# Stick-breaking and gate projections in blocks of four heads, tokens in rows

## What is computed

```python
u = _rms(h, norm1_w[l]) * (1.0 + scale1) + shift1
proj = u @ w_in[l].astype(f32)
qa, ka, va, qkv_b, z_b, b_b, a_b, gate_a, gate_b = jnp.split(proj, IN_OFFSETS, axis=-1)

qa = _rms(_heads_2(qa, SB_HEADS, SB_HEAD_DIM), q_norm_w[l])     # 16 heads of 128
ka = _rms(_heads_2(ka, SB_HEADS, SB_HEAD_DIM), k_norm_w[l])
va = _heads_2(va, SB_HEADS, SB_HEAD_DIM)
o_a = _merge_heads(_stick_breaking(qa, ka, va))

qkv_b = jax.nn.silu(_causal_depthwise_conv(qkv_b, conv_w[l]))
qb, kb, vb = jnp.split(qkv_b, (D_GDN_K, 2 * D_GDN_K), axis=-1)  # l2norm of qb and kb follows
o_b = _gated_delta_rule(qb, kb, vb, g, beta)
o_b = _rms(o_b, o_norm_w[l]) * jax.nn.silu(_heads_2(z_b, GDN_HEADS, GDN_V_DIM))

merged = (jax.nn.sigmoid(gate_a) * (o_a @ p_a[l]) + jax.nn.sigmoid(gate_b) * (o_b @ p_b[l]))
h = h + gate1 * (merged @ w_out[l])
```

## Time and profile before

| | |
|---|---|
| median of 3 timed runs | 2782.45 us (2782.1 to 2784.94) |
| the profiled execution | 2780.33 us |
| its span in the profile | 2778.5 us |
| PE busy | 2753.2 us, 99% |
| DVE, ACT, POOL busy | 74%, 52%, 14% |
| mean granted clock of PE | 0.999 |
| HBM read over the span | 612.70 MB, 222 GB/s |

### The profile page before, as it was taken

How to read it: one execution, slowest core, us unless ns; L and a number is a source line. 1 busy time by engine, 2 the same in 40 slices (tenths; PEclk the granted TensorE clock), 3 DMA queues, 4 the chain that set the end, 5 groups by cost and what they waited for, 6 DMA issues and landing times.

```text
span 2778.5 us, 42932 instructions
## 1 busy us (share of the span) xinstructions
PE 2753.2 (99%) x16354; PEld 2384.8 (86%) x16354; DVE 2049.2 (74%) x3589; ACT 1455.5 (52%) x2414; POOL 378.8 (14%) x958
## 2 busy tenths in 40 slices
PE   8999999999999999999999999999999999999999
PEld 4778888888888888888888888888888888888888
DVE  4478877878988787887878877878978555555554
ACT  3465544555566666666666544444454443444443
POOL 0014300000002424344343311000000000000000
PEclk9999999999999999999999999999999999999999
DMA  9956677788755455555555677887858555555554
GB/s 355 354 179 224 228 248 257 275 288 294 279 183 194 163 175 179 176 185 169 178 172 183 220 244 269 310 289 274 280 175 292 188 188 188 193 185 192 186 198 142
DMA packets 179998, 621.84 MB, mean 224 GB/s; under 512 B 20288, under 2 KB 28752, under 8 KB 179152
## 3 DMA queue, kind: packets, MB, share of 16 engines
q1 hardware_dynamic: 169776, 605.62, 63.5%
q10 hardware_dynamic: 10016, 13.47, 1.5%
HBM read 612.70 MB, written 4.21 MB: 222 GB/s over the span
## 4 chain that ended last, share of the span: by engine, by line
PE 84%; DVE 6%; POOL 3%; ACT 3%; issue 2%; DMA 1%; SPq 0%; ACTq 0%; DVEq 0%
PE ps L101 84%; POOL small L116 2%; DVE wlo L116 2%; POOL small L119 1%; PE ps L104 1%; DVE c_y L122 1%; DMA raw<-in_w_s 1%; ACT sb_l L107 1%; ACT whi L107 1%; ACT L110 1%; DMA xc<-in_xc 0%; DVE acc L122 0%; ACT sb_z L107 0%; DVE i_t L116 0%; DVE c_y L119 0%
## 5 line engine op out<-in xcount | busy, mean ns | idle before, releaser
L101 PE MATMUL ps<-act,whi 128*128 128x512 f32 (+1 forms) x6560 | 1612.4, 392 | 1.2 <-DVE act L116 1.2
L101 PEld LDWEIGHTS ps<-act,whi 128*128 128x128 f32 (+1 forms) x6560 | 1191.1, 188 | 230.2 <-issue 5.7
L116 DVE TENSOR_TENSOR wlo<-raw,whi 128x1024 fp32r<-128x1024 f32 (+3 forms) x883 | 1041.7, 1187 | 18.9 <-ACT whi L107 14.4
L107 ACT ACTIVATE whi<-raw 128x1024 fp32r<-128x1024 f32 (+3 forms) x883 | 893.2, 1026 | 167.9 <-PE ps L101 101.5
L101 PE MATMUL ps<-act,wlo 128*128 128x256 f32 (+2 forms) x6416 | 930.8, 290 | 0.2 <-DVE wlo L116 0.2
L101 PEld LDWEIGHTS ps<-act,wlo 128*128 128x128 f32 (+1 forms) x6416 | 836.9, 190 | 37.5 <-issue 9.2
L122 DVE SCALAR_TENSOR_TENSOR acc<-raw,c_act,acc 128x1024 f32<-128x1024 f32 x210 | 268.5, 1279 | 0.0
L119 POOL TENSOR_SCALAR small<-small 128x2 f32<-128x2 f32 (+3 forms) x316 | 137.6, 435 | 935.0 <-DVE small L119 808.8
L116 POOL TENSOR_TENSOR small<-small 128x2 f32<-128x2 f32 (+1 forms) x460 | 162.9, 354 | 348.3 <-ACT u_u L107 314.1
L116 DVE TENSOR_TENSOR w_u<-w_u,ps 128x256 f32<-128x256 f32 x44 | 18.4, 421 | 94.6 <-ACT w_u L107 94.6
L122 DVE SCALAR_TENSOR_TENSOR h_res<-ps,mod,h_res 128x256 f32<-128x256 f32 x64 | 30.9, 484 | 67.6 <-PE ps L101 66.5
(11 more groups left out here) (328 smaller groups left out, 2295.0 us busy)
## 6 DMA issues: line engine op xcount, KB each, us to landing
raw<-in_w_turns SPq DMA_DIRECT2D x754, 512.0 KB, 4.3
raw<-in_w_mods SPq DMA_DIRECT2D x224, 512.0 KB, 4.3
raw<-in_w_s SPq DMA_DIRECT2D x64, 512.0 KB, 6.7
raw<-in_w_turns SPq DMA_DIRECT2D x64, 448.0 KB, 4.3
raw<-in_w_turns SPq DMA_DIRECT2D x32, 384.0 KB, 3.6
raw<-in_w_turns SPq DMA_DIRECT2D x17, 256.0 KB, 3.1
raw<-in_w_kv SPq DMA_DIRECT2D x7, 512.0 KB, 3.4
xc<-in_xc SPq DMA_DIRECT2D x3, 1024.0 KB, 9.6
```

What stands on the lines that cost most here:

```text
L101: return self.e.matmul(*args, **more)
L107: return self.e.activation(*args, **more)
L116: return self.e.tensor_tensor(*args)
```

## The change

The 64 units sq, sk, sv and gz become 16 blocks, bq, bk, bv and bz, each of four heads. A block has eight turns of 128 x 1024 weights again, now two k-tiles of four heads. In them the activations are stationary (128 tokens of L or H) and the weights move, 512 columns at a time, so that tokens come out in rows, the form that the later steps need. Each turn does both halves of the tokens, one ahead of the small matmuls and one behind them (`tokens`), each into its own bank, so that a block holds both banks 7 and 6:

```diff
+        def tokens(turn, half):
+
+            n, u = 16 + turn.t, turn.tiles[0][0]
+            hi, lo, b = HI[n % NH], LO[n % NL], (u.bank, u.other)[half]
+            s = slice(128 * half, 128 * half + 128)
+            e.wait_ge(*on("hi", n))
+            if turn.tiles[0][1] == 0:
+                claim(b)
+            for j, (_, kt) in enumerate(turn.tiles):
+                e.wait_ge(*on(u.rhs, kt))
+                mm(PS[b][:, :], L[:, 0, kt, s], hi[:, 512 * j:512 * j + 512], kt == 0, False)
+                mm(PS[b][:, :], H[:, 0, kt, s], hi[:, 512 * j:512 * j + 512], False, False)
+            e.wait_ge(*on("lo", n))
+            for j, (_, kt) in enumerate(turn.tiles):
+                p = mm(PS[b][:, :], H[:, 0, kt, s], lo[:, 512 * j:512 * j + 512], False, kt == 15)
+            if half:
+                p.then_inc(*tell("pe_gemm", "w_done", n))
+            elif kt == 15:
+                p.then_inc(*tell("pe_block", "first_rows", u.name, u.i))
+            if kt == 15:
+                held[b] = [("rows", u.name, u.i, half)]
...
+            elif turn.block:
+                tokens(turn, 0)
...
+            if turn.block:
+                tokens(turn, 1)
+                continue
```

The order of the stage is new: bk, bq and bv of the first four heads follow one another, and then a block of eight turns alternates with six turns of gq, gk and gv. gq and gk of head 0 go through the late pair of the stage's start instead of sq and sk. The bases of both mixers are set by hand:

```diff
+        block(0, "bk", 0)
...
+        block(rate, "bq", 0)
+        block(rate, "bv", 0)
+        wide = (("bk", 1), ("bz", 0), ("bq", 1), ("bv", 1), ("bk", 2), ("bz", 1), ("bq", 2), ("bv", 2), ("bk", 3), ("bz", 2),
+                ("bq", 3), ("bv", 3), ("bz", 3))
+        for h in range(1, 17):
+            if h <= len(wide):
+                block(rate, *wide[h - 1])
+            else:
+                for _ in range(4):
+                    gate_a(rate)
             if h < 16:
...
+                delta(h, 0)
+                delta(h, 1)
+            delta(h - 1, 2)
...
-        at = e + 19
...
+        at = e + 27
         for h in range(16):
             at = max(self.end("gk", h), at)
             self.base("delta", h, at)
             at += 14
         for h in range(16):
-            self.base("stick", h, (e + 11, e + 20, e + 29, e + 38)[h] if h < 4 else self.end("sk", h) + 3)
...
+            self.base("stick", h, e + ((29, 40, 50)[h] if h < 3 else 62 + 14 * (h - 3)))
```

More of the change, by code:

```diff
@@ L223, in build, with block, delta, gate_a @@
             single(0.5 if n < 12 else 0, "out1", n, (5, 4, 7, 6)[n % 4], "m", src["w_out"][n], two)
[L225 to L228, removed]
+        self.pairs(0, [Unit("g0", x, 5 - x, "raw", range(16), late=x) for x in range(2)], lambda i: w2[48:65:16])
+        ring = itertools.cycle((7, 6))
+        rate = 0.16
+        def block(rate, name, g):
+            first = {"bq": 0, "bk": 16, "bv": 32, "bz": 96}[name] + 4 * g
+            u = Unit(name, g, bank(), "u", range(16))
+            u.other = bank()
+            for k in range(0, 16, 2):
+                self.turn(rate, np.concatenate([w[:, 128 * kt:128 * kt + 128] for kt in (k, k + 1) for w in w2[first:first + 4]], 1),
+                          [(u, k), (u, k + 1)], block=True)
+            self.finish(u)
+        def delta(g, x):
+            single(rate, "g" + "qkv"[x], g, bank(), "u", w2[48 + 16 * x + g], two)
+        gates2 = iter(range(16))
+        def gate_a(rate=0.5):
+            n = next(gates2, None)
+            if n is not None:
+                single(rate, "ga2", n, bank(), "u", w2[112 + n], two)
+        block(0, "bk", 0)
         ba = Unit("ba", 0, 1, "u", range(16))
@@ L294, in build @@
         e = self.end("out1", 15)
-        at = e + 19
+        for x, name in enumerate(("gq", "gk")):
+            u = Unit(name, 0, None, "raw", range(16))
+            u.end = e + 16 + 2 * x
+            self.units[name, 0] = u
+            self.ends.setdefault((name, u.end), []).append(0)
+        at = e + 27
         for h in range(16):
@@ L300, in build @@
         for h in range(16):
-            self.base("stick", h, (e + 11, e + 20, e + 29, e + 38)[h] if h < 4 else self.end("sk", h) + 3)
-            self.base("turned", h, self.end("sv", h) + (2, 6, 7, 2)[min(h, 3)])
-            self.base("key", h, (e + 10, e + 20, e + 25, e + 36)[h] if h < 4 else self.end("sk", h) + 2)
+            self.base("stick", h, e + ((29, 40, 50)[h] if h < 3 else 62 + 14 * (h - 3)))
         self.place_mods()
-        busy = (*(x + y for x in "sg" for y in "qkvz"), "q", "za", "v", "ba")
+        busy = ("gq", "gk", "gv", "q", "za", "v", "ba")
         low = False
         for turn in self.turns:
-            begins = turn.narrow or any(u.name in busy or u.wide or u.late is not None or kt == u.kts[0] for u, kt in turn.tiles)
+            begins = turn.narrow or turn.block or any(u.name in busy or u.wide or u.late is not None or kt == u.kts[0] for u, kt in turn.tiles)
             turn.low_first = low and not begins
-            low = not turn.narrow and not turn.low_first
+            low = not turn.narrow and not turn.block and not turn.low_first
     def place_mods(self):
@@ L799, in pe @@
                 held[0] = [("b_var",)]
-            for h in due(t, "key"):
+            for h in due(t, "stick", -3):
                 claim(4)
[L804 to L819, removed]
+                k, q = KR[:, h, :], QR[:, h % 8, :]
+                for half in range(2):
+                    e.wait_ge(*on("rows", "bk", h // 4, half))
+                e.wait_ge(*on("q_rows", h // 4))
+                for i, x in enumerate((k, q)):
+                    flip(PS[4][:, 256 * i:256 * i + 128], x[:, 0:128])
+                    p = flip(PS[4][:, 256 * i + 128:256 * i + 256], x[:, 128:256])
+                p.then_inc(*tell("pe_stick", "sb_flip", h))
+                held[4] = [("sb_qt", h)]
             for h in due(t, "stick"):
```

289 lines of the change are left out of this document (146 added, 143 removed).

## The result

The changed kernel takes 2785.84 us (median of 20 runs, 2784.07 to 2787.58) against 2782.36 us before (20 runs). The ratio is 1.0014, with a 95% interval of 1.0008 to 1.0021: slower by 0.14%, which is clear of the noise of these runs but within the 0.2% that the prediction called no change. The forecast was 2784 us, with a range of 2766 to 2798. The profiled execution took 2785.39 us with a span of 2783.6.

The account below looks back on a forecast made before the run. The prediction took TensorE's own instructions to bound the kernel. Its terms, −9.0 − 9.4 + 11 + 7 + 1.7 = +1.3 us, on the profiled 2780.33 plus 2.1 for timed runs gave 2784 us, range 2766 to 2798.

Parts of the forecast that it names:

- A: TensorE waits for ScalarE's u copy, queued behind rows copy and exponential chain: about 1.0 us in eleven periods, +11 us.
- B: Block's second half waits for the preceding v unit's bank, held by its join: 0.6 us at twelve blocks, +7 us.
- The block turns: 128 projection turns, twelve matmuls of 512 columns instead of sixteen mixed: 2.72 us, not 2.79; −9.0 us, small end −3.8.
- The small matmuls: Per head, q and k sums and v flips go, four flips of k and q come: −0.59 us, in all −9.4.
- R1: Rival: waits stay small, taps early, join wait 0, u wait at 7.7 us: 2773 us, 2766 if hidden; chance 0.30.
- R2: Rival: VectorE late at the v unit's join, TensorE stands 1.7 us at each of twelve blocks: 2797 us; chance 0.27.
- C: Start, first blocks in succession: second-half copy behind ScalarE's squares, and u copy at E1+53; about 1.0 and 0.7, +1.7 us.
- R3: Rival: on TensorE, fewer matmuls of equal columns save nothing, sum +10.3 us: 2793 us; chance 0.05.

Follow-up runs that it names:

- experiment 1: Changed kernel, but ScalarE copies u out of its bank ahead of the stick-breaking chain instead of behind it: 2787.92 us, ratio 1.0026.
- experiment 2: Changed kernel, but VectorE does a convolution's last two taps at the head of its turn instead of at its end: 2776.50 us, ratio 0.9983.
- experiment 4: Changed kernel with both ScalarE's u copy ahead of the stick-breaking chain and VectorE's last two taps at the turn's head: 2771.99 us, ratio 0.9966.
- experiment 7: Changed kernel with u copy first, taps early, no modulation tile in a block's first turn, second-half copy ahead of the first half's squares: 2771.13 us, ratio 0.9965.
- experiment 6: Changed kernel with the u copy ahead of the stick-breaking chain and no modulation tile in a block's first turn: 2780.61 us, ratio 0.9998.
- experiment 8: Changed kernel, but each block matmul with the low part of the weights is done as two of 256 columns: 2788.95 us, ratio 1.0027.
- experiment 3: Changed kernel, but the modulation tile stands at the end of VectorE's turn, behind the taps: 2785.82 us, ratio 1.0016.
- experiment 5: Changed kernel, but the plan puts no modulation tile into the first turn of a block: 2783.60 us, ratio 1.0006.

## Why the prediction was right, point by point

**The form of the answer.** A gain of TensorE of some 18 us that two waits give back, net +1.3 us: measured a gain of some 14, and +3.5 us between the medians. Both waits stand where they were put, with the releaser that was named (though another engine held it up at E1+44), and both were made to go, A by experiment 1 and most of B by experiment 2. That the two edits together make the kernel faster than before (experiment 4) shows that the waits were the loss.

**The block turns, −9.0 (−3.8 to −9.0).** The quiet turn is right to the nanoseconds, 2.72, but few block turns are quiet. A turn with one small pair in its middle before, the timeline of TensorE around E1+69,

```profile
1019.99 2.00 PE L101 MATMUL ps<-act,whi 128*128 128x512 f32 x8
1021.83 0.38 PE L101 MATMUL ps<-p_m,i_t 128*128 128x128 f32 x2
1021.97 1.19 PE L101 MATMUL ps<-act,wlo 128*128 128x256 f32 x8
1023.00 0.39 PE L101 MATMUL ps<-act,whi 128*128 128x512 f32 x1
```

takes 3.01 us, and a block turn with one such pair after

```profile
1043.86 1.07 PE L101 MATMUL ps<-whi,act 128*128 128x512 f32 x4
1044.76 0.62 PE L101 MATMUL ps<-wlo,act 128*128 128x512 f32 x2
1045.22 0.38 PE L101 MATMUL ps<-v_v,i_x 128*128 128x128 f32 x2
...
1046.83 0.40 PE L101 MATMUL ps<-act,whi 128*128 128x512 f32 x1
```

2.97: 0.04 gained, not 0.07. The four matmuls behind the pair take 1.01 us (1045.36 to 1046.37, in the rows of A above), the four ahead of it 0.90. In the old turn the eight behind the pair lose as well, but less: 1.03 (1021.97 to 1023.00) instead of 0.95. Summed over the stretch in the trace of experiment 7, where hardly any wait disturbs it, from each matmul's start to the next: the old forms lose 237.6 us (512 columns) and 131.2 (256), the new ones take 244.6 and 118.8. That is −5.5 us; the same sum from the trace of experiment 2 gives −6.6, so it is good to about 1 us. The term was mis-sized by 2.4 to 3.5 us by taking the quiet turn for all 128.

**The small matmuls, −9.4.** By the same sums: q sum −6.6, k sum −5.8, flips of v −3.3, flips of k and q +6.9: −8.8. Right.

**A, +11 (8 to 14).** 0.99 a time where 1.0 was forecast, ten times instead of eleven: about 9.9. The chain took 4.43 us from start to end and began 0.20 after the half was complete (1045.22 to 1045.42): 4.63, where 4.65 was forecast. TensorE's 3.69 came out as forecast, too (1045.22 to 1048.66, and 0.25). What the step did not see is what A hid: had it been nothing, the time would not have been 10 us less, since VectorE was next late (experiments 1 and 6). Rival R1 counted A's removal at its full price.

**B, +7 (0 to 20).** 8.6 us of idle time; the time fell by as much when it was taken away, but part of that was the clock (experiment 2). Per block it is 0 to 0.83 without a tile and 1.40 with one. At E1+100 the addition ended 2.27 us after the block's first turn began, where the row gave 2.28, and TensorE came at 1.99 instead of 1.83. The 1.78 at the first block behind a v unit came by ScalarE's chain, a cause that the step did not name: there its size is luck. R2's mechanism, the modulation tile, is real, in the three blocks of twelve where the tile falls into that turn, and its argument against, that only some blocks will meet a tile, decided it. The chain is that of the earlier trace rows, with the same 0.45 between. That VectorE would be done with the taps no earlier than there (1.41 us into the turn) was right in eight of the twelve blocks; in four it was done after 0.8 to 1.2, and in the three of these that ScalarE did not hold up TensorE waited 0.14 or nothing.

**C, +1.7.** 0.71 at E1+22, as forecast in place and nearly in size for its first part. The second part, the u copy at E1+53, made no wait.

**What was not in the sum.** At E1+44 the wait of 1.78 us was followed by a fall of the clock in the changed kernel itself:

```profile
915.00:920.00 5.00, 3.22 (x13) 2.44 (x13) 2.85 (x7) 4.96 (x7) 0.00 (x0) 0.87 0.26 102
920.00:925.00 5.00, 5.00 (x20) 4.06 (x19) 4.89 (x13) 1.95 (x4) 0.00 (x0) 0.79 0.42 118
```

0.13 and 0.21 of 5 us each: 1.7 us of clock, and all of it after the wait, while TensorE was at work. With the taps early (experiment 2) the wait there is 1.24 and the clock stays at 1.00. The sum also left out that the kernel before had 3.0 us of idle time in this stretch, of which 2.1 net went (0.9 stands for `p_m` in both), and that 1.0 us of the modulation sum moved out of the stretch.

The terms as measured, −5.5 − 8.8 + 9.9 + 8.6 + 0.7 + 1.7 − 2.1 − 1.0 = +3.5, stand against 3.2 in the two traces. The forecast was near in part by luck: a gain that was 4.1 us too large, the 3.1 us that were left out on the other side, and waits and clock whose sum, 20.9, was 1.2 more than the 19.7 that was taken. The upper end of the range, 2798, is a small slip: B at 20 and the rest as forecast add up to 2797.

**R3** is refuted by the quiet turn, that of the changed kernel and that of experiment 8.

## What to carry to other kernels

On an engine that is busy 99% of the time, a change that takes instructions off it is worth only what the other engines let it keep: list, for each instruction that it will reach earlier or each bank that it will want sooner, what must have been done by then and on which engine's queue that stands. A step that others wait for belongs ahead of a long chain in its engine's program order, and the read that frees a single buffer at the head of the turn, not at its end. When one of two waits is removed and the time does not move, look for the same idle time under another releaser before giving up the theory: here moving the u copy was worth nothing alone and 4.5 us once the taps were early. And follow a wait one step beyond the engine that the view names: the join at E1+44 is put down to VectorE, which itself stood waiting for ScalarE.

## What the runs showed of the hardware

TensorE's granted clock fell to its lower level behind waits of 1.12 and 1.40 us that stood 2.1 us apart (experiment 1, at 1218 and 1221 us), and came back within some 6 us; the period lost 2.4 us beside the waits themselves, and 1.2 at E1+72. The same pair at E1+184 left the clock at 1.00, and so did a single wait of 1.40 us (experiment 6, where the pairs had stood). Behind a single wait of 1.78 us, at E1+44, it fell in the changed kernel and lost 1.7 us, and so it did in experiments 1, 3, 5 and 6 (1.78 to 2.37); in experiment 8, behind 1.77 in the same place, it did not. So in these traces the price of a wait is not its length alone, and not the same each time: two that fall together can cost as much again. What decides it is not shown.

The Trainium skill, page "TensorE: Matmul & The Clock Gate", section "A second HAM failure mode: psum-queue depth-cycling", tells of a kernel whose short idle times between groups of matmuls made the clock go between its two levels. Experiment 1 agrees with that at two of its three pairs.

A matmul of 512 columns starts 227 ns after the one before in a stream of its like, and 230 where matmuls of 256 columns stand between (and experiment 8: 0.92 us for four). Those 3 ns and the cost of more instructions are what the blocks gained from. Where small matmuls stand in the middle of a turn, part of it is lost: 0.04 us gained in the turn with one pair, 0.07 in the quiet one.
